# Routed expert rows: where head 16's rows of u are gathered and dotted

## The reference, cut to what matters

```python
q = (xt @ w_q).reshape(TOKEN_BLOCK, PEER_HEADS, 2, PEER_HALF_DIM)
sc = einsum('thcd,chnd->thcn', q, sub_keys)
top_s, top_i = lax.top_k(sc, k)                 # 16 of 128, for both halves
cand_s = top_s[:, :, 0, :, None] + top_s[:, :, 1, None, :]
best_s, best_pos = lax.top_k(cand_s.reshape(...), k)
idx = take_along_axis(cand_i.reshape(...), best_pos)
g = jax.nn.softmax(best_s, axis=-1)
pre = einsum('td,thkd->thk', xt, u[idx])
coef = g * gelu(pre)
return einsum('thk,thkd->td', coef, v[idx])
```

## Time and profile before

| what | value |
| --- | --- |
| median of 3 runs | 2217.22 us (2216.04 to 2224.32) |
| the profiled execution | 2211.96 us |
| its span, first to last instruction | 2209.8 us |
| mean granted TensorE clock in it | 0.913 |
| PE busy | 1933.6 us, 88% |
| DVE busy | 1383.1 us, 63% |
| POOL busy | 965.9 us, 44% |
| ACT busy | 546.6 us, 25% |
| moved by DMA | 614.85 MB, 278 GB/s over the span |

### The profile page before, as it was taken

One profiled execution on the slowest core, in us unless ns is written; L12 is line 12 of the kernel. 1 busy time (PEld: TensorE's weight loads), 2 busy tenths in 40 slices (PEclk: granted clock), 3 DMA queues, 4 the chain that ended last, 5 costly groups with the idle time before them and its releaser, 6 DMA issues.

```text
span 2209.8 us, 22141 instructions
## 1 busy us (share of the span) xinstructions
PE 1933.6 (88%) x7602; PEld 1232.6 (56%) x7602; DVE 1383.1 (63%) x3090; ACT 546.6 (25%) x1520; POOL 965.9 (44%) x814
## 2 busy tenths in 40 slices
PE   6999999887998997867788688999999999986777
PEld 5677666575865665545557576544467544432232
DVE  1111224455888874768986688999689966544544
ACT  2112024412111110213432157401058400011111
POOL 2000000010335572575653266534868875456776
PEclk9999998787998889986799789999999999997879
DMA  6322244155977797897778687899998999999998
GB/s 175 130 96 96 114 158 152 70 188 185 330 276 243 260 333 276 284 378 284 253 273 302 248 302 232 274 354 358 404 390 304 352 409 409 409 361 354 391 380 344
DMA packets 190623, 614.85 MB, mean 278 GB/s; under 512 B 18096, under 2 KB 18096, under 8 KB 190512
## 3 DMA queue, kind: packets, MB, share of 16 engines
q0 software_dynamic: 111168, 403.64, 50.2%
q1 hardware_dynamic: 76400, 202.92, 24.9%
q10 hardware_dynamic: 2944, 6.89, 0.9%
HBM read 610.22 MB, written 3.15 MB: 278 GB/s over the span
## 4 chain that ended last, share of the span: by engine, by line
PE 65%; DVE 11%; DMA 7%; POOL 5%; issue 5%; ACT 4%; another core or an unknown queue 3%; ACTq 0%; POOLq 0%; SPq 0%; DVEq 0%
PE ps L1734 64%; POOL sb_arena L658 5%; DVE sb_arena L1208 4%; DMA sb_arena<-in_peer_u,sb_idx 3%; ACT sb_arena L1035 1%; DMA sb_wring<-in_w_out 1%; DMA sb_gains<-in_norm_g 1%; DMA sb_arena<-in_peer_v,sb_idx 1%; DVE sb_arena L1670 1%; DMA sb_wring<-in_w_in 1%; DMA sb_wring<-in_w_up_attn 1%; PE ps L2052 0%; ACT sb_poolw L1026 0%; DVE sb_arena L1344 0%
## 5 line engine op out<-in xcount | busy, mean ns | idle before, releaser
L658 POOL DMA_INDIRECT sb_arena<-in_peer_u,sb_idx x470 | 616.0, 1311 | 1026.6 <-DVE sb_idx L1197 520.0
L1734 PE MATMUL ps<-sb_wring,sb_arena 128*128 128x512 f32 (+2 forms) x1632 | 701.0, 591 | 43.3 <-DVE sb_arena L1572 18.7
L1208 DVE CUSTOM_DVE_ANT_0 sb_arena<-sb_arena 128x1024 f32<-128x1024 f32 x470 | 562.6, 1221 | 112.3 <-DMA sb_arena<-in_peer_u,sb_idx 108.8
L1734 PEld LDWEIGHTS ps<-sb_wring,sb_arena 128*128 128x128 f32 x1632 | 313.5, 193 | 420.2 <-issue 367.3
L1734 PE MATMUL ps<-sb_arena,sb_wring 128*128 128x256 f32 (+2 forms) x2688 | 518.4, 355 | 22.0 <-issue 10.4
L1734 PEld LDWEIGHTS ps<-sb_arena,sb_wring 128*128 128x128 f32 x2688 | 452.6, 201 | 76.7 <-issue 16.7
L1734 PE MATMUL ps<-sb_arena 128*128 128x64 f32 (+9 forms) x1968 | 337.1, 321 | 40.7 <-ACT sb_arena L920 11.7
L1734 PEld LDWEIGHTS ps<-sb_arena 128*128 128x128 f32 (+4 forms) x1968 | 269.0, 194 | 104.2 <-issue 62.2
L1734 PE MATMUL ps<-sb_arena,sb_poolw 128*128 128x512 f32 (+1 forms) x424 | 206.6, 626 | 65.1 <-issue 34.2
L658 POOL DMA_INDIRECT sb_arena<-in_peer_v,sb_idx x192 | 211.1, 1099 | 119.2 <-issue 47.8
L1237 DVE SCALAR_TENSOR_TENSOR sb_arena<-sb_arena,sb_coef 128x1024 f32<-128x1024 f32 x90 | 115.7, 1285 | 120.4 <-DMA sb_arena<-in_peer_v,sb_idx 101.0
(11 more groups left out here) (240 smaller groups left out, 1362.5 us busy)
## 6 DMA issues: line engine op xcount, KB each, us to landing
sb_wring<-in_peer_v SPq DMA_DIRECT2D x128, 512.0 KB
sb_wring<-in_w_in SPq DMA_DIRECT2D x52, 1024.0 KB, 7.2
sb_wring<-in_peer_w_q SPq DMA_DIRECT2D x32, 1024.0 KB, 6.7
sb_wring<-in_w_o SPq DMA_DIRECT2D x16, 1024.0 KB, 6.6
sb_wring<-in_w_out SPq DMA_DIRECT2D x8, 1024.0 KB
sb_arena<-in_peer_u,sb_idx POOLq DMA_INDIRECT x470
sb_arena<-in_x ACTq DMA_DIRECT2D x8, 512.0 KB, 7.1
sb_wring<-in_w_up_pool SPq DMA_DIRECT2D x4, 1024.0 KB
```

The lines of the kernel that those rows point to most:

```text
L658: nc.gpsimd.indirect_dma_start(gathered[buf(n)], None, table, bass.IndirectOffsetOnAxis(ap=idx[:, t, at_:at_ + 1], axis=0))\
L1208: nc.vector.tensor_tensor_reduce(out=gathered[buf(n)], in0=gathered[buf(n)], in1=xn[:, t % TG, :], scale=1.0, scalar=0.0, op0=ALU.mult, op ...
L1734: return nc.tensor.matmul(o, l, r, start=start, stop=stop)
```

## The change

The 16 `u` rows of head 16 stand ahead of the dense tiles in the list and go through the 6 early buffers, as those of heads 0 to 15. The keys' buffers take first the rows of head 17 and its neighbours. On DVE the routing of heads 16 and 17 is followed by the 16 dots of head 16, then by the split into ranks and `early_over`, then by the routing of heads 18 and 19; the dots no longer stand ahead of the first build. `split()` waits for 272 used rows and 17 chunks' indices (`LATE` and `EARLY_CHUNKS`). What is computed is the same; the new name `DENSE_CHUNKS` keeps the old count where it means the chunks of the dense tiles. From head 17's first row on, order and buffers are as before.

```diff
--- before.py
+++ after.py
@@ -51,7 +51,8 @@
 SW = 2048
 UNITS = 129
 EARLY_BUFS = 6
-EARLY_CHUNKS = 16
+DENSE_CHUNKS = 16
+EARLY_CHUNKS = 17
 LAG = 2
 EDGE = TOPK // 2
 SUMS = TOPK + (TOPK - 1) * EDGE
@@ -493,7 +494,7 @@
         LATER = [("u", k) for k in range(27, CHUNKS)] + [("v", 19)]
         LAST = range(20, CHUNKS)
         order_of_dmas = [row for k in range(EARLY_CHUNKS) for row in head("u", k)]
-        order_of_dmas += [("d", i, 0) for i in range(NK)] + head("u", 16)
+        order_of_dmas += [("d", i, 0) for i in range(NK)]
         order_of_dmas += [row for b in range(BUILDS) for row in beside_first(b)]
         order_of_dmas += [row for k in WITH_TILES for row in head("u", k)]
         order_of_dmas += [row for b in range(BUILDS) for row in beside_second(b)]
@@ -501,7 +502,7 @@
         order_of_dmas += [row for k in LAST for row in head("v", k)]
         place = {row: n for n, row in enumerate(order_of_dmas)}
         GATHERS = len(order_of_dmas)
-        assert GATHERS == len(place) == CHUNKS * TOPK + (CHUNKS - EARLY_CHUNKS) * TOPK + NK
+        assert GATHERS == len(place) == CHUNKS * TOPK + (CHUNKS - DENSE_CHUNKS) * TOPK + NK
         LATE = EARLY_CHUNKS * TOPK
         ROWS = LATE + NK
         OPEN = place["v", LAST[0], 0]
@@ -510,7 +511,7 @@
             return k == 19 or k not in (V_FIRST, V_SECOND) and j % 2 == 1
 
         v_at, taken = {}, {False: 0, True: 0}
-        for k in range(EARLY_CHUNKS, CHUNKS):
+        for k in range(DENSE_CHUNKS, CHUNKS):
             for j in range(TOPK):
                 v_at[k, j] = taken[on_vector(k, j)]
                 taken[on_vector(k, j)] += 1
@@ -520,8 +521,7 @@
 
         tile_ring = list(RING)[2:]
         row_ring = list(KEYS) + list(RING)[:2]
-        opening = list(KEYS) + list(range(4)) + list(RING)[:2]
-        turned = (OPEN - ROWS - len(opening)) % len(row_ring)
+        turned = (OPEN - ROWS) % len(row_ring)
         last_ring = row_ring[turned:] + row_ring[:turned] + list(SCORES) + list(OVER) + tile_ring
 
         def buf(n):
@@ -529,10 +529,8 @@
                 return n % EARLY_BUFS
             if n < ROWS:
                 return tile_ring[(n - LATE) % len(tile_ring)]
-            if n < ROWS + len(opening):
-                return opening[n - ROWS]
             if n < OPEN:
-                return row_ring[(n - ROWS - len(opening)) % len(row_ring)]
+                return row_ring[(n - ROWS) % len(row_ring)]
             return last_ring[(n - OPEN) % len(last_ring)]
 
         uses, count_of, had, seen = {}, {}, {}, {}
@@ -1243,9 +1241,9 @@
                     dve.wait_ge(d_used, NK)
                     dve.wait_ge(x2_back, 16 * TG)
                 else:
-                    dve.wait_ge(v_used, sum(not on_vector(k, j) for k in range(EARLY_CHUNKS, H * t + H)
+                    dve.wait_ge(v_used, sum(not on_vector(k, j) for k in range(DENSE_CHUNKS, H * t + H)
                                             for j in range(TOPK)))
-                mine = sum(on_vector(k, j) for k in range(EARLY_CHUNKS, H * t + H) for j in range(TOPK))
+                mine = sum(on_vector(k, j) for k in range(DENSE_CHUNKS, H * t + H) for j in range(TOPK))
                 if t >= TG:
                     dve.wait_ge(vector_used, mine)
                 if t:
@@ -1268,13 +1266,13 @@
                     yield from dots(k)
                 for k in range(1 + H // 2, 2 * H):
                     yield from dots(k)
+                yield from tops_of(2 * H, 2 * H + 1)
+                yield from dots(DENSE_CHUNKS)
                 split()
                 early_over[0] = True
-                yield from tops_of(*range(2 * H, 2 * H + 4))
+                yield from tops_of(2 * H + 2, 2 * H + 3)
                 while not dense_over[0]:
                     yield
-                for _ in dots(16):
-                    pass
                 beside = chain(*[dots(k) for k in U_FIRST])
                 for b in range(BUILDS):
                     picks(b)
```

## The result

The changed kernel took 2232.37 us in the median of 21 runs, the kernel before 2221.15 us in 21 runs beside them. The ratio is 1.0039, with a 95% interval of 1.0020 to 1.0058: 8.7 us slower (4.4 to 12.9). The forecast was +8.6. The two medians are further apart, 11.2 us; the median forecast from the three runs shown was 2226, and 3.9 of the 6.4 us by which it was missed are a kernel before that stands at 2221.15 over 21 runs, not at 2217.22.

The account below looks back on a forecast made before the run. PE's stages from the first build on store nothing up, so the build's start sets the end. DVE's later coefficients add +11.1 us, a smoother build −2.5: +8.6, median 2226 us, own range 2220 to 2231, wider range 2214 to 2236.

Parts of the forecast that it names:

- DVE's chain now ends last: Before the first build: coefficients ready at 1300.1, after PE's products at 1288.8, so DVE alone sets the start.
- The sum to the build: Head 16's indices to first build: dots, split, routing, weighing and ACT's steps; start at 1306.4 against 1295.28, +11 us.
- Split: Three small DVE operations moved behind head 16's dots, now on the path: 0.9 us.
- weighing: DVE's weighing of 16 heads stays behind the routing: 5.60 us, coefficients ready at 1300.1.
- rival A: Full pauses: routing of heads 18 and 19 takes its 24.15 us again; typically +15, 2232 us; chance 0.20.
- The term for the dots: Head 16's dots, paced by 6 buffers and POOL: first at 1248.3, 8.1 us after its gather, over at 1275.
- The term for the pauses: Routing of heads 18 and 19 after the dots: 18.5 us, somewhat under half of its 9.7 us of pauses recurring.
- The smoother start of the build: First build: a DVE wait of 2.50 us may go with head 17's rows sent earlier; −2.5 us, bounds 0 and −3.8.
- B: Quick return of rows, routing in 14.4 us, coefficients before 1289.0: about −4 us, 2213 us; chance 0.15.
- C: Later stages give the delay back because DMA worked ahead: 2217 plus or minus 2 us; chance 0.10.
- D: Gathers ahead of the ranks start the build earlier by the dots' 18.7 us: 2199 us; chance 0.03.
- One sign of being wrong: Head 16's gathers beginning well before 1240 us would show the forecast wrong.

Follow-up runs that it names:

- mixed: Changed kernel with the routing of heads 18 and 19 run between head 16's dots; ratio 0.9995 to the kernel before.
- own16: Changed kernel with 16 buffers for head 16's rows, the 10 keys' and 6 early ones, all free from the start; ratio 1.0056 to the kernel before.
- hold_weights: Against own16, SP loads the last four pieces of tile 3's query weights only after head 16's dots; one execution, dots end 30.7 us after the indices.
- before_again: The kernel before, unchanged, run again for a second trace on another chip; ratio 0.998, 48.9 us from index cast to first build.

## Why the prediction was right, step by step

**That DVE's chain now ends last: right.** PE waits 8.88 us for the coefficients, and where the routing was put back under the waits (mixed) the loss went. DVE's idle time from the indices to the last dot is 18.4 us in all, where I had 16 to 19.

**The sum to the build: right in total, by two terms that missed in opposite directions.** Forecast 66.7 us from the indices, measured 66.6 (64.7 in the mean of three traces). The dots were to end 35.3 us after the indices and ended 38.4 us after them (mean of three 36.6); the routing was to take 18.5 and took 15.2. Split 0.9, weighing 5.6 and the 6.3 us to the build came as read. That +8.6 met +8.7 so closely is luck in part: the first trace of the kernel before was the slow one of three in this stretch, and −2.5 us of the sum did not come. So is it that the measured median, 2232, is the number of rival A; my narrower range, 2220 to 2231, just misses it.

**The term for the dots: near in size, wrong in its cause.** I had the first row 8.1 us after its gather, and then 6 buffers and POOL's pace. The first dot came 4.5 us after the gather, with none ahead of it. The last eight came each 2.05 us, with six buffers or 16 and with POOL done or not, because SP's weights take over a third of full DMA engines (own16, hold_weights); only 5 us of the dots' time is shown to hang on that. The DMA queues in the windows of the two rows that I read would have pointed there: the dots 2.05 us apart (955 to 962, first two lines) and the gather that took 8.1 us (977 to 987, last two lines) stood beside SP's loads, with 29.1 and 71.8% of the engines:

```profile
q0 software_dynamic: 556, 2.04, 74.0%
q1 hardware_dynamic: 396, 0.78, 29.1%
...
q1 hardware_dynamic: 1177, 2.61, 71.8%
q0 software_dynamic: 264, 0.95, 24.0%
```

I also read all 16 gathers of the kernel before as sent in one run; 14 were. It cost the sum nothing, since the dots wait only 0.21 us for the last two. The 2.0 us plus bytes of the Trainium skill ("DMA: Bandwidth & Descriptors", "Anatomy of one DMA — SWDGE (gpsimd) path") give, as an estimate, 3.2 us for a gather; the trace has 4.5 from the issue to the first dot. The estimate is nearer than my 8.1 for the first row; it is for one DMA, and the later rows are not to be had from it.

**The term for the pauses: wrong.** I let 4.1 of their 9.7 us come back. They came in none of the changed kernel's three traces, and in one of three of the kernel before. The Trainium skill ("Runtime: NRT & Kernel Launch", "Instruction fetch mechanics"), which I set against them, has the cost of code loading mostly hidden. Five of these six traces have no pause, which agrees; whether code loading made the pauses of the sixth no run shows. The paused trace also stood under the base: 55.6 us to the build where two others have 49. So over three traces each the change costs 13.6 us of that stretch rather than 11. The second ratio is +13.6 us too (7 to 20). The first is +8.7, and its upper end, 12.9, lies just below.

**The smoother start of the build: too large.** −2.5 forecast, −0.5 measured (111.8 to 111.3); over all traces of both kernels it is 111.0 to 111.9.

**Rivals.** A (full pauses) had the pauses wrong. B (not slower) failed: coefficients 60.1 us after the indices, not before 49 (its −1 − 3.8 is −4.8, so 2212 and not 2213). C (absorbed later): the tile stages are equal to 0.1 us and nothing was given back. D: the gathers do not begin earlier from the indices on. One sign of being wrong came by chance: head 16's first gather went out at 1232.94, well before 1240. The cast spreads over 1231 to 1240 us in both kernels (the table), and the gather follows it by 0.45 us as before.

## What to carry to other kernels

Work that stands between a request and its use is cover. Before moving the use forward, write down what will run in the wait; here 15 us of routing and 6 of weighing went from under the gathers to behind them. If the use must move, move the cover with it, piece by piece (mixed). And read a stretch in more than one trace before its pauses become a term of a sum.

## What the runs showed of the hardware

- Two queues that both have work moved equal numbers of packets through full DMA engines, 720 and 721 in 10 us (own16), with 66.2 and 37.0% of the engines. By its bytes the gathers' queue moved 512 KB each 2.0 us; with SP's loads held back, each 1.6 us (hold_weights).
- The first gather of a burst was dotted 4.5 us after its issue, one beside loads that had 71.8% of the engines 8.1 us after the earlier trace rows.
- Between groups of runs the whole kernel differed by more than the change: the kernel before had a median of 2221.15 us in the first and 2187.55 in the group of before_again, with 260.7 against 243.7 us in the last stage and a mean granted clock of 0.913 against 0.935. What makes the groups differ no run shows.
